# Repeating a chunk's gate rows on all partitions: one fp32 product, or one fp32r product of stacked high and low parts

## What is computed

```python
b = jnp.cumsum(fc, axis=-1)
Dm = jnp.where(tril, b[..., :, None] - b[..., None, :] + ic[..., None, :], -jnp.inf)
inter = b + m[..., None]
m_t = jnp.maximum(inter, jnp.max(Dm, axis=-1))
wD = jnp.exp(Dm - m_t[..., None])
sqk = jnp.einsum('bhtd,bhsd->bhts', qc, kc) * wD
```

## Time and profile before

| | |
|---|---|
| median of 3 runs | 1005.39 us (1004.89 to 1005.7) |
| the profiled execution's own time | 1003.45 us |
| its span, first to last instruction | 1001.8 us |
| granted TensorE clock, mean | 0.984 of full |
| busy: PE, PEld | 940.2 us (94%), 758.2 us (76%) |
| busy: DVE, ACT, POOL | 494.1 us (49%), 391.8 us (39%), 109.6 us (11%) |
| moved by DMA | 142.36 MB, 142 GB/s |

### The profile page before, as it was taken

One profiled execution on the slowest core, in us unless ns is written; L12 is line 12 of the kernel. 1 busy time (PEld: TensorE's weight loads), 2 busy tenths in 40 slices (PEclk: granted clock), 3 DMA queues, 4 the chain that ended last, 5 costly groups with the idle time before them and its releaser, 6 DMA issues.

```text
span 1001.8 us, 18453 instructions
## 1 busy us (share of the span) xinstructions
PE 940.2 (94%) x6951; PEld 758.2 (76%) x6951; DVE 494.1 (49%) x1082; ACT 391.8 (39%) x841; POOL 109.6 (11%) x236
## 2 busy tenths in 40 slices
PE   4999999999999999999799999998878999999996
PEld 3989989999978888887566667765557786677774
DVE  4642745554564444543466655556454533433222
ACT  5442354323424543333654544445453222431211
POOL 1300000000000000001100014342011000000000
PEclk9999999999999999999999999999888999999998
DMA  7361215222242222221987679977974522203221
GB/s 223 96 171 43 63 44 150 68 58 63 64 136 71 84 75 62 74 79 36 369 271 209 225 251 339 344 248 226 311 260 165 212 94 80 62 15 134 72 91 43
DMA packets 115265, 142.36 MB, mean 142 GB/s; under 512 B 9623, under 2 KB 75799, under 8 KB 115178
## 3 DMA queue, kind: packets, MB, share of 16 engines
q1 hardware_dynamic: 109418, 122.31, 38.3%
q0 software_dynamic: 5760, 18.88, 5.5%
HBM read 125.34 MB, written 15.41 MB: 140 GB/s over the span
## 4 chain that ended last, share of the span: by engine, by line
PE 83%; DMA 4%; DVE 4%; ACT 3%; SPq 3%; issue 2%; POOL 1%; POOLq 0%; ACTq 0%; DVEq 0%
PE ps L1946 73%; PE ps L1949 10%; DMA Vr<-in_cache_v 2%; DMA xrow<-in_x_prompt 1%; SPq L574 1%; DMA Kr<-in_cache_k 1%; SPq L570 1%; PE ps L1941 1%; DVE pp L1760 0%; DMA wst<-in_w_in 0%; POOL small L729 0%; ACT U L923 0%; ACT wh L939 0%; ACT junk L1221 0%; POOL small L726 0%
## 5 line engine op out<-in xcount | busy, mean ns | idle before, releaser
L1946 PE MATMUL ps<-hhi,whi 128*128 128x272 f32 (+1 forms) x672 | 227.5, 338 | 1.2 <-DVE hlo L1286 1.2
L1946 PE MATMUL ps<-hhi,wlo 128*128 128x272 f32 (+1 forms) x672 | 218.0, 324 | 0.0
L1946 PE MATMUL ps<-hlo,whi 128*128 128x272 f32 (+1 forms) x672 | 217.6, 324 | 0.0
L1946 PE MATMUL ps<-wh,r 128*128 128x512 f32 (+1 forms) x544 | 155.0, 401 | 0.1
L1946 PEld LDWEIGHTS ps<-hhi,whi 128*128 128x128 f32 x672 | 127.9, 190 | 14.2 <-issue 4.1
L1946 PEld LDWEIGHTS ps<-hlo,whi 128*128 128x128 f32 x672 | 127.9, 190 | 9.9 <-issue 1.9
L1946 PEld LDWEIGHTS ps<-hhi,wlo 128*128 128x128 f32 x672 | 127.6, 190 | 9.3
L1946 PEld LDWEIGHTS ps<-wh,r 128*128 128x128 f32 (+1 forms) x544 | 99.3, 185 | 26.2 <-issue 1.0
L1302 DVE TENSOR_TENSOR wlo<-wst,whi 128x1024 fp32r<-128x1024 f32 x56 | 69.2, 1236 | 84.4 <-ACT whi L898 84.3
L1725 DVE COPY kTs<-ps 128x512 f32<-128x512 f32 x64 | 44.1, 689 | 65.3 <-PE ps L1949 65.2
L1949 PEld LDWEIGHTS ps<-ident,Kr 128*128 128x128 f32 x512 | 56.2, 141 | 24.3 <-issue 22.5
(11 more groups left out here) (344 smaller groups left out, 1399.5 us busy)
## 6 DMA issues: line engine op xcount, KB each, us to landing
Kr<-in_cache_k SPq DMA_DIRECT2D x128, 256.0 KB, 4.1
wst<-in_w_in SPq DMA_DIRECT2D x56, 512.0 KB, 3.9
Vr<-in_cache_v POOLq DMA_DIRECT2D x72, 256.0 KB, 4.6
Vr<-in_cache_v SPq DMA_DIRECT2D x56, 256.0 KB, 4.1
out_y_prompt<-rows SPq DMA_DIRECT2D x16, 512.0 KB, 2.9
xrow<-in_x_prompt SPq DMA_DIRECT2D x8, 512.0 KB, 5.1
wout<-in_w_out SPq DMA_DIRECT2D x8, 512.0 KB, 5.6
rows<-in_x_prompt SPq DMA_DIRECT2D x8, 512.0 KB, 4.3
```

The source lines that it names most:

```text
L1946: return nc.tensor.matmul(out, lhsT, rhs, start=start, stop=stop, **more)
```

## The change

Row A is split like the operands of the projection. DVE copies row A, rounded to fp32r, into row 1 of `gat` through a second view of the same memory (`gat_r`), and writes the rest, row A less that copy, into row 3 of `gat`. The high part goes into the blocks of `Ablk` on partitions 0 to 3, the low part into the same blocks on partitions 32 to 35; the partitions between stay zero. `Ablk` and `ones` become fp32r tensors, and one fp32r product over 36 rows, instead of one fp32 product over 128, leaves high plus low part on all partitions.

The new operations sit on DVE between the last scan results and `aL`: a copy of 4x128, a subtraction of 4x128 and a second block product of 4x512. Two new waits (`row_split`) order the copy before the subtraction and the subtraction before the second block. The copy into `G` is written behind the first copy. `aL` still completes the twelfth count. The count `kvtok_ready`, on which nobody waited, is dropped, and its semaphore is used for `row_split`. The other users of `ones` read it through a view as fp32.

```diff
-        ones = sb("ones", [P, P])
+        ones_r = sb("ones", [P, P], F32R)
+        ones = ones_r[:, :].bitcast(F32)
...
-                      ("kw", [P, H, DH]), ("Ablk", [P, H, P]), ("gat", [H, 5, P]), ("G", [P, P]), ("wqk", [P, H, DH]),
+                      ("kw", [P, H, DH]), ("Ablk", [36, H, P], F32R), ("gat", [H, 5, P]), ("G", [P, P]), ("wqk", [P, H, DH]),
...
+            before_gat = sum(4 * math.prod(shape[1][1:]) + 31 & ~31 for shape in shapes[:[n for n, *_ in shapes].index("gat")])
+            buffers = {name: place(f"{name}{hf}", *shape) for name, *shape in shapes}
+            buffers["gat_r"] = place(f"gat_r{hf}", [H, 5, P], F32R, offset=first + before_gat)
+            return buffers
...
-                nc.gpsimd.memset(z[:], 1.0 if z is vaug_[0] else 0.0).then_inc(s["zero_ready"], 1)
+                nc.gpsimd.memset(z[:].bitcast(F32) if z is Ablk_[0] else z[:], 1.0 if z is vaug_[0] else 0.0).then_inc(s["zero_ready"], 1)
...
                 dve.wait_ge(s["gate_step"], gs0 + 9)
+                row_r, row_lo = gat_r_[hf][:, 1, :], gat[:, 3, :]
                 if i >= 1:
                     dve.wait_ge(s["AB_ready"], i)
                 if i == H:
                     dve.wait_ge(s["zero_ready"], 18 + 3)
-                gstep(nc.vector.tensor_tensor(Ablk[0:H, :, :], lead(gat[:, 0, :], H), bc(ident[0:H, 0:H], P), ALU.mult))
+                nc.vector.tensor_copy(row_r, gat[:, 0, :]).then_inc(s["row_split"], 1)
                 gstep(nc.vector.tensor_copy(G[0:H, :], gat[:, 4, :]))
+                dve.wait_ge(s["row_split"], 2 * i + 1)
+                nc.vector.tensor_tensor(row_lo, gat[:, 0, :], row_r.bitcast(F32), ALU.subtract
+                                        ).then_inc(s["row_split"], 1)
+                nc.vector.tensor_tensor(Ablk[0:H, :, :], lead(row_r.bitcast(F32), H), bc(ident[0:H, 0:H], P), ALU.mult)
+                dve.wait_ge(s["row_split"], 2 * i + 2)
+                gstep(nc.vector.tensor_tensor(Ablk[32:32 + H, :, :], lead(row_lo, H), bc(ident[0:H, 0:H], P), ALU.mult))
                 gstep(nc.vector.tensor_copy(aL, gat[:, 0, P - 1:P]))
...
                 for h in range(H):
-                    last = turn(ps[:, 4, h * P:(h + 1) * P], x[h])
-                last.then_inc(s["kvtok_ready"], 1)
+                    turn(ps[:, 4, h * P:(h + 1) * P], x[h])
...
-                mm(ps[:, 7, P:P + H], ones[:, :], Dg[:, :]).then_inc(s["GT_ready"], 1)
-                mm(ps[:, 5, :], ones[:, :], Ablk[:, :, :].rearrange("p h t -> p (h t)")).then_inc(s["AB_ready"], 1)
+                mm(ps[:, 7, P:P + H], ones, Dg[:, :]).then_inc(s["GT_ready"], 1)
+                mm(ps[:, 5, :], ones_r[0:36, :], Ablk[:, :, :].rearrange("p h t -> p (h t)")).then_inc(s["AB_ready"], 1)
```

More of the change, by code:

```diff
@@ L12 @@
+import math
 import concourse.bass as bass
@@ L290, in chunk_buffers @@
                 shapes.remove(("wq", [P, H, DH]))
-            return {name: place(f"{name}{hf}", shape) for name, shape in shapes}
+            before_gat = sum(4 * math.prod(shape[1][1:]) + 31 & ~31 for shape in shapes[:[n for n, *_ in shapes].index("gat")])
+            buffers = {name: place(f"{name}{hf}", *shape) for name, *shape in shapes}
+            buffers["gat_r"] = place(f"gat_r{hf}", [H, 5, P], F32R, offset=first + before_gat)
+            return buffers
         half_buffers = [chunk_buffers(0, u1_base)]
@@ L303, in program @@
             for name in ("E", "nd", "vaug", "qbT", "kw", "Ablk", "gat", "G", "wqk", "wkv", "xch", "wg"))
+        gat_r_ = [b["gat_r"] for b in half_buffers]
         wvT = kw_[0]
@@ L416, in program @@
             scores_ready s_stored negmax_ready p_ready coef_ready ao_ready ao_step
-            gates_ready kvtok_ready sqk_ready gate_step gate_exp rows_exp GT_ready
+            gates_ready row_split sqk_ready gate_step gate_exp rows_exp GT_ready
             AB_ready gt_stored kw_ready arg_ready E_ready W_ready inter_ready intra_ready nd_scaled
@@ L714, in _ @@
             nc.gpsimd.memset(ident[:, :], 0.0).then_inc(s["zero_ready"], 1)
-            nc.gpsimd.memset(ones[:, :], 1.0).then_inc(s["zero_ready"], 1)
+            nc.gpsimd.memset(ones, 1.0).then_inc(s["zero_ready"], 1)
             nc.gpsimd.memset(mhalf, -0.5).then_inc(s["zero_ready"], 1)
@@ L803, in _ @@
             for z in (Ablk_[1], G_[1], vaug_[1]):
-                nc.gpsimd.memset(z[:], 1.0 if z is vaug_[1] else 0.0).then_inc(s["zero_ready"], 1)
+                nc.gpsimd.memset(z[:].bitcast(F32) if z is Ablk_[1] else z[:], 1.0 if z is vaug_[1] else 0.0).then_inc(s["zero_ready"], 1)
             for i in range(H, CH):
@@ L2053, in _ @@
             turn(ps[0:SMP, 5, 0:P], G[:, 0:SMP])
-            mm(ps[:, 5, P:P + SMP], ones[:, :], DgS[:, :, :].rearrange("p h b -> p (h b)")).then_inc(*signal["s_GT"])
+            mm(ps[:, 5, P:P + SMP], ones, DgS[:, :, :].rearrange("p h b -> p (h b)")).then_inc(*signal["s_GT"])
             mm(ps[0:SMP, 7, 0:P], ones[:, 0:SMP], AblkS[:, :, :].rearrange("p h t -> p (h t)")).then_inc(*signal["s_AB"])
```

## The result

The changed kernel takes 1007.2 us (median of 20 runs, 1004.14 to 1010.93) and the kernel before 1005.05 us (20 runs, 1001.52 to 1007.0). The ratio is 1.0028 with a 95% interval of 1.0015 to 1.0041: slower by some 2.8 us (1.5 to 4.1; the two medians lie 2.15 apart), where 1.0 us faster was forecast (1004.4, range 1001.8 to 1006.9). These repeat to 0.03 us within each trace, with one exception (in twice36, explained there), and the totals only confirm them.

A forecast was written before the change was run, and what follows sets the result against it. PE was taken to bound the kernel, with the gate chain on the path only in chunks 0 to 3. +1.72 - 2.84 + 0.15 = -0.97, called -1.0 us, from a median of 1005.39 gave 1004.4; 8-in-10 range 1001.8 to 1006.9.

The forecast's parts named there:

- What bounds the kernel: PE bounds both prompt stretches; gate chain on the path in chunks 0 to 3, about 2.28 us slack in 4 to 7.
- The added DVE work, 1.14 us: DVE's gate chain: aL starts 1.88 us after the chain's start instead of 0.74; bounds 0.94 to 1.27.
- held and overlapping operations: DVE's low block and aL: each held until earlier operations finish (delay 1.14 us), or both overlapping (0.94).
- The product, saving 0.71 (bounds 0.63 to 0.75): PE's Ablk product: fp32r takes 0.23 us instead of 0.94, saving 0.71 per chunk, 5.7 over eight.
- the 0.08 that the lower bound named: Old Ablk product on PE: one of its two records carries 0.08 us that needn't go, so saving 0.63.
- The product isn't faster: Rival, PE's Ablk product: 36 rows in fp32r still take 0.94 us; +4.6 us, 1010.0; chance 0.02.
- The clock rival: Longer PE stops before G, chunks 0 to 3, halve the clock, 1.5 us per fall; 1007.4 to 1010.4; chance 0.09.
- Never reaches PE: Rival: the longer gate chain doesn't delay PE, so all eight savings count; 999.8 us; chance 0.11.
- DVE overlaps after all: Rival: DVE's low block and aL overlap earlier operations, delay 0.94 us; -1.8 us, 1003.6; chance 0.14.
- What is late next: After the product, chunks 4 to 7: E's weighting keeps 0.20 of 0.91 us slack; chunk 4's weight tile has only 0.56.
- The 0.15 charged: Chunk 4's weight tile: slack of 0.56 us loses 0.15 of the 0.71 saved.
- The sum: Whole kernel: +1.72 (chunks 0 to 3) - 2.84 (chunks 4 to 7) + 0.15 = -0.97 us, called -1.0.

The follow-up runs named there:

- twice36: Changed kernel with the 36-row fp32r product issued twice in a row; per chunk 35.71 us (0 to 3) and 37.30 (5 to 7), product stretch 1.32.
- dve_only: Changed kernel's DVE work, with the product left in fp32 over 128 rows; ratio to the kernel before 1.0047 (1.0028 to 1.0065).
- rows128: Changed kernel with Ablk and ones on all 128 partitions in the fp32r product; ratio to the kernel before 0.9996 (0.998 to 1.0012).
- fp32_36: Kernel before with only its fp32 Ablk product over 36 rows instead of 128; per chunk 34.47 us (0 to 3) and 37.69 (5 to 7).

## Why the prediction was wrong, point by point

- **What bounds the kernel.** Right: PE, with a stop before G in chunks 0 to 3 and slack in 4 to 7.
- **The added DVE work, 1.14 us.** Right to the hundredth, in the changed kernel (1.88 to aL) and in dve_only (35.32); that it is so exact is in part luck, since one step was 0.03 shorter than priced and three were 0.01 longer. The choice between held and overlapping operations was right too: the low block starts at 156.84, the end of the high one, and aL 0.04 behind the end of the low one. By the Trainium skill's rule (VectorE: DVE Perf Modes, "Two Vector instructions with no wait between them") both should be held, and this trace agrees. The new wait between the two blocks is not what holds the second: the subtraction has such a wait ahead of it too and still starts at 155.96, 0.07 before the copy into G ends. No run here has the low block on partition 0 for comparison.
- **The product, saving 0.71 (bounds 0.63 to 0.75).** This step failed. Measured: 0.34. It was priced by rows of products whose neighbours also use 128 rows, and the range took 36 rows as something that could only help: the prediction put the passage between row counts at nothing. 0.27 of the 0.37 missing is the passage from 128 rows to 36 and back (rows128 gets it back; fp32_36, without fp32r, loses 0.29 by it; twice36 pays it once for two products). The other 0.10 is that even among 128-row products the saving is 0.61. In rows128 the new product's record lasts 0.48 where those behind it last 0.40, and the next product starts 0.32 behind it where the following ones have 0.24; in twice36 the second of the two products, too, starts 0.34 behind the first. So the first fp32r product behind the fp32 ones has a surplus of nearly 0.1. It is about the 0.08 that the lower bound named in the old product's first record; whether it is the same thing no run shows.
- **The rivals.** "The product isn't faster" named the right term and gave it 0.02, as all or nothing, with the row of another row count as the argument against it. It needed a middle: half the gain. The clock rival did not come true in the profiled execution of the changed kernel: the stops of 1.1 us left the granted clock at 1.00 in both stretches, as this table shows. It can't be dismissed for every execution, since twice36 has one fall of 1.5 us behind such a stop; at one in 24 it would add, as an estimate, 0.25 us to an execution with four stops. "Never reaches PE" failed: dve_only has the whole 1.14 in each of chunks 0 to 3. "DVE overlaps after all" failed by the starts at 156.84 and 157.56.

```profile
145.00:280.00 135.00, 130.71 (x1048) 127.55 (x1048) 71.85 (x173) 46.80 (x130) 8.37 (x12) 1.00 0.27 75
320.00:465.00 145.00, 145.00 (x767) 122.62 (x766) 76.03 (x173) 59.71 (x120) 8.11 (x10) 1.00 0.24 70
```

- **What is late next.** Nothing was, at this size: with 0.36 gained a chunk, chunk 4's weight tile (slack 0.56) and E's weighting (0.91) kept their cover: from chunk 4's turn of G to chunk 5's it went from 48.30 to 47.94, the same 0.36. The 0.15 charged was not paid.
- **The sum.** With 0.34 in place of 0.71 the same working gives 4 x (1.14 - 0.34) - 4 x 0.34 = +1.8, what the trace has. The sign hung on one price: the break-even lies at half of 1.14, 0.57 a product, between the measured price and the predicted one.

The Trainium skill (TensorEngine Tiling (Array Packing), "Key Properties") says that a change of tiling mode drains TensorE, and (same page, "When to Use Tiling") it ties row tiling to contractions of at most 64. The Trainium skill doesn't say that an ordinary product of few rows counts as such a change. Read that way it would have spoken against this change of the kernel, and the prediction didn't weigh it. The runs fit that reading: 36 and 64 rows pay 0.27 us for the passage in and out together, 100 and 128 rows don't. That a mode is what changes is not in the trace; it shows row counts, weight loads and times.

## What to carry to other kernels

Price a matmul by rows that share its row count with their neighbours: a lone product of 36 or 64 rows among full ones cost about 0.27 us beyond its columns, and padding it with zero rows to 100 or 128 was cheaper than leaving them out. When an edit puts work between two operations of a chain, look who waits for the second one and move it ahead of the new work: with 128 rows, aL first turned a time level with before (0.9996) into a gain of 0.45%. The changed kernel's loss of 0.28% turns by both together: by the distances with 36 rows (33.71 and 37.06) the order alone would bring it to some 3.3 us under the kernel before, and the padding does the rest. And where a forecast is a small difference of two large terms (4.6 against 5.7 us), give the chance to the sign only after asking of each term what would halve it.

## What the hardware showed that was not expected

- Passing from 128-row products to one of 36 or 64 rows and back costs 0.27 us in fp32r (1.08 against 0.81) and 0.29 in fp32 (1.71 against 1.42); about 0.07 of it stands ahead of the product (0.21 against 0.14 behind the small one) and 0.2 behind it, where in fp32r the next weights are no longer loaded under the running product. With 100 rows it is nothing (0.80).
- A 512-column fp32 product among full-row ones takes 0.61 us more than one in fp32r (1.42 against 0.81), not the 0.71 that the pace of uniform fp32r products gives.
- A stop of PE of 1.1 us was followed once in 24 times by 3 us at half the granted clock, 1.7 us after PE had resumed (twice36, chunk 2); the other 23 kept 1.00. What tells them apart isn't shown.
